# Eight output tiles laid into the state-space chunks of a two-block model, its skip term on TensorE, reordered latent heads, and one stage for convolution and z

## The reference

```python
# latent attention, per head: q_nope, q_rope, k_nope, k_rope, v from latents; rope on q
s = q_nope @ k_nope.T + q_rope @ k_rope.T        # scaled, causal, softmax
o = softmax(s) @ v ; y = o * silu(gate)

# even layer of the second block
y_a = rmsnorm(diff_attention(q, k, v), subln_w) * (1 - lambda_init) * silu(g_a)
xbc = silu(causal_dwconv(xbc, conv_w, conv_b))   # xs, bm, cm
dt  = softplus(dt_raw + dt_bias)
y   = ssd_scan(xh, dt, A, bm, cm)                # 8 chunks of 128 tokens, 16 heads of 64
y   = y + xh * d_skip                            # the skip term
y   = y * silu(z)
y_b = rmsnorm(y in 2 groups of 512, ssd_norm_w)
x   = x + concatenate([y_a, y_b]) @ w_out
```

## Time and profile before

| | us |
|---|---|
| median of 3 runs | 2910.68 (2908.81 to 2911.7) |
| the profiled execution, its own time | 2906.41 |
| its span in the trace | 2904.6 |
| TensorE busy | 2579.6 (89%) |
| VectorE busy | 1629.3 (56%) |
| ScalarE busy | 1212.9 (42%) |
| GpSimd busy | 202.8 (7%) |

### The profile page before, as it was taken

One profiled execution on the slowest core, in us unless ns is written; L12 is line 12 of the kernel. 1 busy time (PEld: TensorE's weight loads), 2 busy tenths in 40 slices (PEclk: granted clock), 3 DMA queues, 4 the chain that ended last, 5 costly groups with the idle time before them and its releaser, 6 DMA issues. The chain is left out here.

```text
span 2904.6 us, 32337 instructions
## 1 busy us (share of the span) xinstructions
PE 2579.6 (89%) x11997; PEld 2112.5 (73%) x11997; DVE 1629.3 (56%) x2882; ACT 1212.9 (42%) x2053; POOL 202.8 (7%) x121
## 2 busy tenths in 40 slices
PE   5999698979989798999999979987767897999978
PEld 4777487867777576888888867776556686888856
DVE  6655464435454457666666664522883364666654
ACT  4555432224444443555555543412442233554432
POOL 0000020000000052000000000001320030000012
PEclk9999799989999999999999989998777999999998
DMA  2221421221212131011111102224423331011133
GB/s 100 71 71 69 138 89 50 73 94 59 80 51 87 65 110 51 30 37 37 37 37 37 37 15 73 101 76 146 128 87 109 102 94 40 30 43 36 37 116 109
DMA packets 89970, 206.99 MB, mean 71 GB/s; under 512 B 7152, under 2 KB 39792, under 8 KB 88816
## 3 DMA queue, kind: packets, MB, share of 16 engines
q1 hardware_dynamic: 89840, 205.25, 21.2%
HBM read 164.26 MB, written 40.96 MB: 71 GB/s over the span
## 5 line engine op out<-in xcount | busy, mean ns | idle before, releaser
L144 PE MATMUL acc<-operand_hi,w_hi 128*128 128x512 f32 x1958 | 795.0, 406 | 71.9 <-DVE w_lo L139 13.1
L146 PE MATMUL acc<-operand_hi,w_lo 128*128 128x512 f32 x1958 | 773.1, 395 | 0.0
L145 PE MATMUL acc<-operand_lo,w_hi 128*128 128x512 f32 x1958 | 772.2, 394 | 0.0
L144 PEld LDWEIGHTS acc<-operand_hi,w_hi 128*128 128x128 f32 x1958 | 373.5, 191 | 159.6 <-issue 58.4
L146 PEld LDWEIGHTS acc<-operand_hi,w_lo 128*128 128x128 f32 x1958 | 373.0, 191 | 81.8
L145 PEld LDWEIGHTS acc<-operand_lo,w_hi 128*128 128x128 f32 x1958 | 374.1, 191 | 75.0 <-issue 2.6
L133 ACT ACTIVATE w_hi<-w_raw 128x1024 fp32r<-128x1024 f32 (+1 forms) x209 | 202.6, 969 | 432.0 <-PE aux L146 184.5
L139 DVE TENSOR_TENSOR w_lo<-w_raw,w_hi 128x1024 fp32r<-128x1024 f32 (+1 forms) x209 | 233.1, 1115 | 217.8 <-ACT w_hi L133 217.5
L144 PE MATMUL aux<-operand_hi,w_hi 128*128 128x512 f32 x522 | 213.2, 408 | 64.1 <-DVE w_lo L139 35.9
L146 PE MATMUL aux<-operand_hi,w_lo 128*128 128x512 f32 x522 | 208.9, 400 | 0.0
L145 PE MATMUL aux<-operand_lo,w_hi 128*128 128x512 f32 x522 | 208.8, 400 | 0.0
(11 more groups left out here) (395 smaller groups left out, 4353.9 us busy)
## 6 DMA issues: line engine op xcount, KB each, us to landing
w_raw<-in_stream SPq DMA_DIRECT2D x209, 512.0 KB, 3.6
ssd_e<-cs_scratch SPq DMA_DIRECT2D x8, 1024.0 KB, 4.8
g_scratch<-conv_y SPq DMA_DIRECT2D x12, 512.0 KB, 2.9
ssd_xbc<-g_scratch SPq DMA_DIRECT2D x8, 768.0 KB, 6.1
y_scratch<-rnn_y SPq DMA_DIRECT2D x10, 512.0 KB, 3.1
out_a_raw<-y_scratch SPq DMA_DIRECT2D x20, 256.0 KB, 6.3
resid<-in_x SPq DMA_DIRECT2D x8, 512.0 KB, 7.2
g_scratch<-mlai_g SPq DMA_DIRECT2D x8, 512.0 KB, 2.9
```

Source lines behind the costliest of these rows:

```text
L144: pe.matmul(out, w_hi, x_hi, start=first, stop=False)
L145: pe.matmul(out, w_hi, x_lo, start=False, stop=False)
L146: return pe.matmul(out, w_lo, x_hi, start=False, stop=last)
```

## The change

1. The output projection of the differential heads leaves `project_scratch`, which is gone, and is made inside `ssd_chunks`. Its operands are loaded and split in chunk 0, through three buffers that the chunk work uses later (`hd`, `yt`, half of `yy`). Tile b-1 is made in round b: first token half in two quarters of 12 products (`early`, `late`), then the second half in two, all in one PSUM bank `pu`, so a half begins when VectorE has added the other to the residual (`added`). The last tile follows the last round.
2. The carried product is made in two halves through one bank `po`.
3. The skip term becomes 8 products on TensorE, which start the accumulation of the product within the chunk: x times a diagonal `dg` that GpSimd makes once. GpSimd's skip product and VectorE's skip addition are gone.
4. ScalarE copies the turned output; the norm's weight is applied when the scan's output is split for its own projection (`gain`). The norm of a chunk is applied a round later, and the by-token copies of the next chunk stand at the end of ScalarE's round.
5. Convolution and z share one block; their programs stand one behind the other.
6. In the latent heads, `values` of a pair of blocks stands one block later, `pth` has two buffers, both turns of block 6 stand inside the key projection, the values are turned behind their projection, and the rotation works in place and frees its bank after its third operation. The first head's rotated query is split earlier.

The diff, cut to its core (indentation shortened):

```diff
-        pe.wait_ge(s["pth"], PIECES * b + n)
-        pe.wait_ge(s["y"], 4 * b + t // 2)
+        pe.wait_ge(s["pth"], PIECES * b + piece_at(t))
+        pe.wait_ge(s["y"], 4 * b + (t - 1) // 2)
...
-    pe.wait_ge(s["pth"], PIECES * b + (piece_at(2 * g_ + 2) if g_ < 3 else PIECES))
+    pe.wait_ge(s["pth"], PIECES * b + (piece_at(2 * g_ + 3) if g_ < 3 else PIECES))
...
+                turn(b, t, piece)
         if t == 0 and b:
             values(b - 1, 3)
+        if t in (3, 5, 7):
+            values(b, t // 2 - 1)
         if t == 1:
-            turn_values(b)
             if more:
                 units("v", b + 1)
-        if t in (2, 4):
-            values(b, t // 2 - 1)
+            turn_values(b)
         if t == 2 and more:
             units("r", b + 1)
         if t == 3 and more:
             units("q", b + 1)
         if t == 6:
             if more:
-                units("k", b + 1)
-            values(b, 2)
+                units("k", b + 1, whole)
+            else:
+                whole()
+            continue
         turn(b, t, parts[0])
-        def rest():
-            for piece in parts[1:]:
-                turn(b, t, piece)
         if t == 0:
             scores(b, 1)
             scores(b, 2)
         elif t < 6:
             scores(b, t + 2, rest)
-        elif t == 7 and more:
-            scores(b + 1, 0, rest)
         else:
             rest()
+            if more:
+                scores(b + 1, 0)
 values(last, 3)
...
-    rope_dve(dve, s, b, proj("r", b), rope, t12, k.acc_free[t.slot])
-    dve.wait_ge(k.acc_free[t.slot], t.before + 1)
-    dve.tensor_tensor(t12[:, 0, :], t12[:, 0, :], t12[:, 1, :], ALU.add).then_inc(s["rot"], 1)
+    acc = proj("r", b)
+    dve.tensor_tensor(t12[:, :], acc[64:128, :], rope[64:128, :], ALU.mult).then_inc(s["ra"], 1)
+    dve.tensor_tensor(acc[0:64, :], acc[0:64, :], rope[0:64, :], ALU.mult).then_inc(s["rb"], 1)
+    dve.wait_ge(s["ra"], b + 1)
+    dve.wait_ge(s["rb"], b + 1)
...
-    conv_tiles(k)
-    step_sizes_and_z(k, tab)
+    with ExitStack() as c:
+        conv, steps = conv_tiles(k, c), step_sizes_and_z(k, c, tab)
+        with k.nc.Block(no_gpsimd_drain=True) as block:
+            @block.sync
+            def _(sp):
+                conv.sp(sp)
+                steps.sp(sp)
...
+    load_y(d)
 load_x(1)
 load_c(1)
+load_y(3)
+load_ahead(sp, k, j0, 0, 2, 0)
 for b in range(QT):
     if b < last:
         sp.wait_ge(s["tz"], b + 1)
         load_z(b + 1)
+    if not b:
+        load_y(4)
+        load_y(5)
     if b + 2 < QT:
-        sp.wait_ge(s["cb"], b + 1)
-        if b:
-            sp.wait_ge(s["yo"], b)
+        sp.wait_ge(s["yd"], b + 1)
         load_x(b + 2)
-        sp.wait_ge(s["yd"], b + 1)
         load_c(b + 2)
-    if b:
-        sp.wait_ge(s["yt"], b)
...
+        load_y(7)
+    else:
+        load_ahead(sp, k, j0, b, 2, 0)
+        store(b - 1)
...
+    t = tile(j)
+    if kts[0] == 0:
+        if n:
+            pe.wait_ge(s["added"], j + 1)
+        else:
+            wait_tile(pe, k, t)
+            if j:
+                pe.wait_ge(k.acc_free[tile(j - 1).slot], tile(j - 1).before + 1)
+    for kt in kts:
+        if not j and not n:
+            pe.wait_ge(s["ylo"], kt + 1)
+        w = slice(kt * P, (kt + 1) * P)
+        mm = three_passes(pe, pu, k.w_hi_sb[:, t.slot, w], k.w_lo_sb[:, t.slot, w],
+                          bank(k.xh[:, kt, :], n), bank(k.xl[:, kt, :], n), kt == 0, kt == DT - 1)
+    if kts[-1] == DT - 1:
+        mm.then_inc(k.tile_done[t.slot] if n else s["first"], 1)
+early, late = range(DT // 2), range(DT // 2, DT)
 front(0)
...
     if b:
-        pe.wait_ge(s["h"], b)
-        if b >= 2:
-            pe.wait_ge(s["y1"], b - 1)
-        for g in range(2):
-            mm = pe.matmul(bank(po, g), x[:, 10 + g, :], bank(h[:, :], g), start=True, stop=True)
-        mm.then_inc(s["yo"], 1)
+        carried(b, 0)
+        project(b - 1, 0, early)
+        carried(b, 1)
...
-        d = slice(n * HD, (n + 1) * HD)
-        mm = pe.matmul(px[:, d], e[:, b % 2, n, :], xdt[:, d], start=True, stop=True)
+    pe.wait_ge(s["dg"], 1)
+    for t in range(DT):
+        pe.matmul(px[:, t * P:(t + 1) * P], x[:, t, :], dg[:, t, :], start=True, stop=False)
+        for n in (2 * t, 2 * t + 1):
+            d = slice(n * HD, (n + 1) * HD)
+            mm = pe.matmul(px[:, d], e[:, b % 2, n, :], xdt[:, d], start=False, stop=n % 2 == 1)
     mm.then_inc(s["yd"], 1)
+    if b:
+        project(b - 1, 0, late)
     pe.wait_ge(s["zs"], b + 1)
     if b:
         turn_output(b - 1)
+        project(b - 1, 1, early)
     if b < last:
         front(b + 1)
+    if b:
+        project(b - 1, 1, late)
+project(last, 0, range(DT))
 pe.wait_ge(s["yt"], last)
 turn_output(last)
+project(last, 1, range(DT))
...
     act.activation(tz[:, :], pz, ACT.Tanh, scale=0.5).then_inc(s["tanh"], 1)
+    if b:
+        split_hi(act, k, tile(b))
+    else:
+        operand(1)
+        operand(2)
     if b < last:
...
+    if b:
+        output(b - 1)
     act.wait_ge(s["v"], b + 1)
     act.activation(st[:, b % 2, 2, :], st[:, b % 2, 1, :], ACT.Sqrt).then_inc(s["sd"], 1)
+    if b < last:
+        by_token(b + 1)
+    if not b:
+        for d in (6, 7):
+            operand(d)
+split_hi(act, k, tile(QT))
...
                            ).then_inc(s["xdd"], 1)
     if 0 < b < last:
         pool.wait_ge(s["h"], b)
+        if b == 1:
+            pool.wait_ge(s["ylo"], DT)
         pool.tensor_tensor(heads(hd[:, :]), heads(h[:, :]), head_col(b, 4), ALU.mult).then_inc(s["hd"], 1)
-    pool.tensor_tensor(heads(xs[:, :]), heads(xs[:, :]), d, ALU.mult).then_inc(s["xd"], 1)
...
+def carried(b, g):
+    y_g = bank(yy[:, b % 2, :], g)
+    dve.wait_ge(s["yo"], 2 * (b - 1) + g + 1)
+    if b >= 2 and not g:
+        dve.wait_ge(s["turned"], b - 1)
...
+    if b:
+        carried(b, 0)
+    else:
+        operand(0)
     dve.wait_ge(s["tanh"], b + 1)
     if b:
         dve.wait_ge(s["yy"], b)
     dve.scalar_tensor_tensor(out=zs[:, :], in0=tz[:, :], scalar=1.0, in1=pz,
                              op0=ALU.add, op1=ALU.mult).then_inc(s["zs"], 1)
+    if b:
+        carried(b, 1)
+        norm(b - 1)
+    else:
+        operand(1)
+        operand(2)
     if b < last:
         dve.wait_ge(s["st"], b + 1)
         if b:
             dve.wait_ge(s["hd"], b)
-            dve.wait_ge(s["yo"], b)
+            dve.wait_ge(s["yo"], 2 * b)
...
-        differences(b + 1)
+        split_lo(dve, k, tile(b))
+    else:
+        for d in (3, 4, 5):
+            operand(d)
     dve.wait_ge(s["yd"], b + 1)
     if b:
-        dve.wait_ge(s["y1"], b)
+        dve.wait_ge(s["y1"], 2 * b)
         dve.tensor_tensor(y, px, y, ALU.add).then_inc(s["y2"], 1)
-        dve.wait_ge(s["y2"], b + 1)
-        dve.wait_ge(s["xd"], b + 1)
...
-        dve.tensor_tensor(y, y, xs[:, :], ALU.add).then_inc(s["y3"], 1)
-    dve.wait_ge(s["y3"], b + 1)
+    dve.wait_ge(s["y2"], b + 1)
     dve.wait_ge(s["zs"], b + 1)
     dve.scalar_tensor_tensor(out=y, in0=y, scalar=0.5, in1=zs[:, :],
                              op0=ALU.mult, op1=ALU.mult).then_inc(s["yy"], 1)
     if b:
-        output(b - 1)
+        added(b - 1, 0)
+    variance(b)
     if b < last:
         causal(b + 1)
-    dve.wait_ge(s["sq"], 2 * b + 2)
-    v, sd, r, u = (st[:, b % 2, n, :] for n in range(1, 5))
...
+added(last - 1, 1)
+split_lo(dve, k, tile(QT))
+added(last, 0)
+added(last, 1)
...
-project_scratch(k, "out_da", 0, DT, False)
-project_halves(k, "out_ssd", DT, DT, "c2")
+project_halves(k, "out_ssd", DT, DT, "c2", gain="ssd_norm")
```

619 lines of the change are left out of this document (319 added, 300 removed).

## The result

The changed kernel takes 2815.82 us (median of 4 runs, 2811.24 to 2823.59), the kernel before beside it 2911.19 us (2908.81 to 2912.71): a ratio of 0.968, 95% interval 0.9666 to 0.9695. The prediction said 2813, within 2787 to 2845. The profiled execution took 2814.39 us with a span of 2812.6, 92.0 less than the one before.

What follows compares the result with a forecast made beforehand. Chunk rounds were taken as bound by a loop through VectorE, at clock 0.72. Savings of 67.2 + 14.5 + 16 = 97.7 us turn the profiled 2906.4 into 2808.7, as median 2813 us, range 2787 to 2845.

Steps and rivals of the forecast that it cites:

- A round: Steady chunk round after the change: TensorE's work sums to 23.1 us; with waits, 24.2 us was taken.
- the worse order: Chunk round, VectorE's wide product and GpSimd's first scaling ready together: in one order TensorE waits 1.0 us for the projection bank.
- No slack on VectorE behind the second carried product: Chunk round: there VectorE owes 7.3 us and TensorE 7.2, so about 0.2 us late.
- The second rival (VectorE bound): Chunk rounds: VectorE becomes the bound, one more GpSimd collision lengthens every round; 7 x 2.5 = 17 us, 2830 us; chance 0.15.
- The first chunk: It gets longer by splitting eight operands: chunk 1's head products end at 2062.6 instead of 2050.9, 52 us after the first turn.
- The tail: Behind the last head products at 2205.6: the stage ends 23.2 us later, the next stage's load comes at 2229.2.
- Chunk stage in all: Chunks with the differential heads' output projection: the next stage's load comes 67.2 us earlier.
- Convolution and z: Between convolution and z: the TensorE gap and half-clock restart go, a 0.5 us wait at the second tile comes; gain 14.5 us.
- latent heads, "the start gives 2, the last head 2": Latent heads: 12 us for seven heads, 2 at the start, 2 in the last head; 16 us in all.
- the head's 1.7: Latent heads, new order of waits: each head 1.7 us shorter, 12 us for seven.
- Third rival, the clock falls at the head products: Chunk rounds: the clock falls within each round as before; 7.8 x 7 = 55 us more, 2868 us; chance 0.09.
- Fourth rival, the single bank: Chunk rounds: TensorE waits for VectorE's additions and stays at half clock; + 22 x 7 = 154 us, 2967 us; chance 0.04.

Runs made afterwards that it cites:

- the two undisturbed traces: Changed kernel with old latent heads and convolution and z in two blocks, 2843.09 us; changed kernel with last head's value products in old places, 2813.98 us.
- the last two experiments: Changed kernel with first chunk's sum ahead of operands 3 to 5, 2812.55 us; the same plus three more reorderings, 2805.5 us.
- the woven part alone: Changed kernel with the old latent heads and convolution and z in two blocks: 2843.09 us, ratio 0.9772 to the kernel before.
- the two other traces of the old heads: Kernel before with only convolution and z in one block, 2892.18 us; changed kernel with old heads and those two in separate blocks, 2843.09 us.
- the two clock experiments: Changed kernel with three quarters of the woven projection's filling left out, 2791.02 us; changed kernel with a TensorE wait of about 5 us put back, 2887.29 us.

## Why the prediction was right, and where it was off

The time and the mechanism were right: the woven projection makes the chunk rounds TensorE's at full clock. By the prediction's own steps:

- **A round.** TensorE's sum 23.1 and the wait of 1.0 in the worse order gave 24.2; measured 24.29, five times within 0.02. The wait is 0.76 to 0.79 and is the one named, at the projection bank, behind the wide product held up by GpSimd. The skip and head products are 5.47 us from first to last, forecast 5.5; without skip products the head products are 3.68, so these cost 1.8, forecast 1.7. The last round took 22.57, forecast 22.0.
- **Two readings that were off, without effect on the sum.** The stretch of the earlier trace rows from 2050.9 holds six rounds, not seven (131.0 / 6 = 21.8). And the GpSimd operation in the earlier trace rows that holds a small VectorE operation for 1.82 us makes `hd`, which stays; the skip scaling that goes held the next one for 1.83.
- **No slack on VectorE behind the second carried product** (7.3 against 7.2). Its sum starts at 2086.88, as the head products end at 2086.84, and the run with an extra operation of 1.21 us there lost 0.56 a round, the one without skip products got back only 0.57 of 1.8. So there is no slack up to the sum; of the extra 1.21 the waits behind it take up 0.65. The second rival (VectorE bound) was near, not far.
- **The first chunk.** Head products of chunk 1 end 51.9 us after the first turn in the two undisturbed traces, forecast 52; in the changed kernel's own trace 53.7, since the state products ran at half clock (3.62 us, for 2.57 and 2.66). The cause given, operands and decays ahead of the sum, is what the last two experiments took away.
- **The tail.** The last addition ends at 2182.26 + 23.2 = 2205.4, as forecast; the load follows 24.4 behind instead of 23.6.
- **Chunk stage in all**: 67.2 forecast, 63.3 in the profile, 65.1 in the woven part alone. The 2.1 are 0.3 of the first chunk (forecast 51.6), 0.6 of the last round, 0.4 of five rounds, 0.8 of the handover. That the norm's gain costs nothing was not tested alone: the stretch behind the chunks took 604.7 to 611.4 us in the three kernels without it and 603.6 to 611.4 in the others.
- **Convolution and z**: 14.5 forecast, 14.8 in the part alone and in the changed kernel, with 0.31 us of waiting at the second tile for 0.5; and 1.5 to 1.8 more because the wait for the first load is shorter. That I had not counted, and what shortens it stays open.
- **The step that failed: latent heads, "the start gives 2, the last head 2".** Counted from one head's border to the next, five heads gave 1.64 us each, forecast 1.7, but the one before the last only 0.5; the first head with the start gave 3.8, of which 1.2 fall ahead of its first scores. Start and seven heads give 12.5, forecast 14. The last head took 2.1 more than in the one profile of before, instead of 2 less, and 0.5 more than in the two other traces of the old heads: the waits that the next head's projections cover elsewhere are open there, and the longest one costs the clock too. The sum is 10.2 in the profile and 10.8 alone, and 11 to 13 against those two traces, for 16.
- **Luck in the head's 1.7.** The waits that the prediction lists for the new order (0.4, 0.75, 1.35, 0.6, 0.1) add up to 3.2 us a head; of the 4.1 before, that saves 0.9, not 1.7. Measured were 0.34, 0.81, 0.98 and 0.17, together 2.3, because the 1.35 came out shorter and the 0.6 ahead of the third value product is not there.
- **Luck in the total.** The profiled execution took 2814.39 us where 2808.7 was forecast for it, 5.7 more; the median is off by 2.8 only, because this kernel's profiled execution lies 1.4 us below its median, where the prediction had added 4.3. The 92.0 us of the trace also hold 2.2 behind the chunks that were not forecast and are within the scatter of that stretch.
- **Third rival, the clock falls at the head products.** It did not, and the two clock experiments say why: no wait of 5 us is left ahead of them. With one put back the rival's picture is there, and dearer: 75.9 us of chunk stage for 55 forecast. Some 34 of them are the waits themselves (38.5 ahead of the head products, less 4.7 at the projection bank).
- **Fourth rival, the single bank.** It costs 0.8 us a round, not 22.

## What to carry to other kernels

Work that one engine alone is bound by belongs into the idle time of that engine in a stage bound by another; it pays twice if the idle time was in waits long enough to halve TensorE's clock. Place it so that the longest single wait gets short, not so that the engine is merely busier: with a quarter of the filling the clock held as well. And check the last iteration of a rotated loop by itself: waits that the next iteration's work hides are open there. Where a small edit is judged, read its stage in the trace: the total moved by up to 8 us for reasons elsewhere.
